# Merging three mixer branches: branch product ahead of its gate, and the branches in another order

## What is computed

```python
def merge_branches(y_pool, y_na, y_mla, g_logits, w_branch, w_out):
    ...
    ys = jnp.stack([y_pool, y_na..., y_mla...], axis=2)
    proj = jnp.einsum('btnc,ncd->btnd', ys, w_branch)
    gates = jax.nn.sigmoid(g_logits.reshape(B, T, N_BRANCHES, D_MODEL))
    return jnp.sum(gates * proj, axis=2) @ w_out
```

## Time and profile before

| what | us |
|---|---|
| median of three runs | 2220.57 (2215.8 to 2220.63) |
| the profiled execution's own time | 2216.48 |
| span of its trace, first to last instruction | 2214.3 |
| TensorE busy in that span | 1944.2 (88%) |

### The profile page before, as it was taken

How to read it: one execution, slowest core, us unless ns; L and a number is a source line. 1 busy time by engine, 2 the same in 40 slices (tenths; PEclk the granted TensorE clock), 3 DMA queues, 4 the chain that set the end, 5 groups by cost and what they waited for, 6 DMA issues and landing times.

```text
span 2214.3 us, 29157 instructions
## 1 busy us (share of the span) xinstructions
PE 1944.2 (88%) x11852; PEld 1507.2 (68%) x11852; DVE 747.4 (34%) x1370; ACT 525.0 (24%) x873; POOL 204.9 (9%) x204
## 2 busy tenths in 40 slices
PE   3799898989999996999718998989899999979990
PEld 1698555668888654888518975656788885558880
DVE  1422657641222135111162227566312122341113
ACT  1311351541111020111142114335311101201113
POOL 0102410010000000100130041100100000001004
PEclk8799999999999998999958999999999999989995
DMA  9413442121132418999672123121213124389985
GB/s 313 161 60 79 156 161 77 58 77 57 58 112 79 124 61 310 358 356 358 227 257 79 69 42 136 39 77 58 77 58 114 58 76 133 131 307 353 359 302 189
DMA packets 183336, 340.97 MB, mean 154 GB/s; under 512 B 12252, under 2 KB 91500, under 8 KB 182892
## 3 DMA queue, kind: packets, MB, share of 16 engines
q1 hardware_dynamic: 152188, 266.16, 34.7%
q10 hardware_dynamic: 23264, 44.96, 6.2%
q0 software_dynamic: 7776, 28.32, 3.6%
HBM read 309.63 MB, written 41.30 MB: 158 GB/s over the span
## 4 chain that ended last, share of the span: by engine, by line
PE 78%; DVE 10%; issue 4%; DMA 3%; ACT 2%; POOL 1%; SPq 0%; ACTq 0%; DVEq 0%; POOLq 0%
PE pair L1491 70%; PE opair L1491 5%; PE pair L1537 3%; DVE mid L1079 1%; DMA r<-mod_rows 1%; DMA ring<-in_w_up 1%; DVE mid L973 1%; DVE mid L975 1%; DVE r L1330 1%; ACT r L879 1%; DVE r_r L1165 1%; DVE mid L1091 0%; DVE mid L1203 0%; ACT mid L846 0%; POOL ysT L1456 0%
## 5 line engine op out<-in xcount | busy, mean ns | idle before, releaser
L1491 PE MATMUL pair<-r_r,mid_r 128*128 128x320 f32 (+2 forms) x2688 | 477.6, 314 | 0.0
L1491 PEld LDWEIGHTS pair<-r_r,mid_r 128*128 128x128 f32 x2688 | 416.6, 189 | 8.8 <-issue 1.5
L1491 PE MATMUL pair<-r,ring 128*128 128x128 f32 (+1 forms) x2432 | 323.6, 294 | 4.5 <-DMA ring<-in_w_up 4.5
L1491 PEld LDWEIGHTS pair<-r,ring 128*128 128x128 f32 x2432 | 299.6, 194 | 38.3 <-issue 15.3
L1491 PE MATMUL pair<-ring,hT 128*128 128x512 f32 (+1 forms) x640 | 231.0, 520 | 5.7 <-DVE hT L1181 3.6
L1537 PE MATMUL pair<-cst,mid 128*128 128x128 f32 (+1 forms) x668 | 106.2, 298 | 122.1 <-DVE mid L975 93.6
L1537 PEld LDWEIGHTS pair<-cst,mid 128*128 128x128 f32 (+1 forms) x668 | 81.1, 151 | 166.4 <-DVE mid L975 97.7
L1491 PEld LDWEIGHTS pair<-ring,hT 128*128 128x128 f32 x640 | 120.4, 190 | 108.5 <-issue 72.7
L1491 PE MATMUL pair<-ysT_r,mid_r 128*128 128x256 f32 (+1 forms) x768 | 171.2, 314 | 11.2 <-issue 11.2
L814 ACT ACTIVATE r<-pair 128x640 f32<-128x640 f32 x48 | 33.7, 703 | 461.9 <-PE pair L1491 461.9
L1491 PE MATMUL pair<-ysT,ring 128*128 128x320 f32 x512 | 143.0, 432 | 0.0
(11 more groups left out here) (230 smaller groups left out, 2137.3 us busy)
## 6 DMA issues: line engine op xcount, KB each, us to landing
ring<-in_w_mod SPq DMA_DIRECT2D x27, 2048.0 KB, 8.9
ring<-in_w_in SPq DMA_DIRECT2D x20, 2048.0 KB, 8.5
ring<-in_w_gate SPq DMA_DIRECT2D x34, 1024.0 KB, 7.3
ring<-in_w_up SPq DMA_DIRECT2D x34, 1024.0 KB, 12.4
ring<-in_w_down SPq DMA_DIRECT2D x34, 1024.0 KB, 11.0
expert_out<-r ACTq DMA_DIRECT2D x34, 512.0 KB, 7.4
ring<-in_w_branch SPq DMA_DIRECT2D x12, 1024.0 KB, 7.4
expert_out<-in_zeros SPq DMA_DIRECT2D x17, 512.0 KB, 12.2
```

The source lines that it names most:

```text
L1491: return nc.tensor.matmul(out, lhsT, rhs, start=first, stop=last, skip_group_check=True)
```

## The change

In each pair TensorE now makes the branch tile first and the gate tile second, and the three branches are taken in the order neighbourhood (1), latent (2), pool (0). The order of the chunks in each group stays gate, then branch. A line was added near the top, so that from there on every line of the new file stands one further down (L814 is L815).

```diff
-MERGE = [(m, n) for c in range(2) for n in range(3) for m in range(4 * c, 4 * c + 4)]
+BRANCHES = (1, 2, 0)
+MERGE = [(m, n) for c in range(2) for n in BRANCHES for m in range(4 * c, 4 * c + 4)]
...
     for m, n in MERGE:
-        jobs += [("gate", m, n), ("branch", m, n)]
+        jobs += [("branch", m, n), ("gate", m, n)]
...
-HALVES += [(("gate", c, n), a, ("gate", 4 * c + 2 * a + 1, n)) for c in range(2) for n in range(3) for a in range(2)]
+HALVES += [(("gate", c, n), a, ("gate", 4 * c + 2 * a + 1, n)) for c in range(2) for n in BRANCHES for a in range(2)]
...
-        for n in range(3):
+        for n in BRANCHES:
             chunks += [(("gate", c, n), None), (("branch", c, n), ("branch", 4 * c + 3, n))]
...
-                await_job(act, ("gate", KD - 1, 2))
+                await_job(act, ("gate", KD - 1, BRANCHES[-1]))
...
-                    out = mergedT[:, m, :] if n == 0 else prod[:, i % 2, :]
+                    out = mergedT[:, m, :] if n == BRANCHES[0] else prod[:, i % 2, :]
...
                     if n == 0 and m == 0:
-                        pe.wait_ge(g_parts_ready, KD)
-                    channels_split(("gate", m, n), HALF_OF[(("gate", m // 4, n), m % 4 // 2)], m % 2 * P, by_channel)
-                    if n == 0 and m == 0:
                         await_read(pe, ("pool", NM - 1))
                     if n == 2 and m == 0:
                         pe.wait_ge(o_freed, 2 * NM)
                     channels(("branch", m, n), wb, (m % 4) * P, NM, yT[n], T, MID)
+                    if n == BRANCHES[0] and m == 0:
+                        pe.wait_ge(g_parts_ready, KD)
+                    channels_split(("gate", m, n), HALF_OF[(("gate", m // 4, n), m % 4 // 2)], m % 2 * P, by_channel)
```

More of the change, by code:

```diff
@@ L565, in _ @@
                             await_mod_stored(sp, n - 1)
-                            await_job(sp, ("gate", KD - 1, 2))
+                            await_job(sp, ("gate", KD - 1, BRANCHES[-1]))
                         for i in range(MT):
@@ L1175, in _ @@
                     await_read(dve, ("gate", m, n))
-                    out = mergedT[:, m, :] if n == 0 else prod[:, i % 2, :]
+                    out = mergedT[:, m, :] if n == BRANCHES[0] else prod[:, i % 2, :]
                     V.tensor_tensor(out, ps[:, MID:MID + T], sig[:, i % 2, :], ALU.mult)\
                         .then_inc(freed[PAIR_OF[("branch", m, n)]], 1)
-                    if n:
+                    if n != BRANCHES[0]:
                         await_read(dve, ("branch", m, n))
                         ins = V.tensor_tensor(mergedT[:, m, :], mergedT[:, m, :], prod[:, i % 2, :], ALU.add)
-                        if n == 2:
+                        if n == BRANCHES[-1]:
                             ins.then_inc(merged, 1)
```

## The result

The changed kernel takes 2224.49 us (median of 9 executions, 2221.05 to 2227.27) against 2217.13 (9 executions, 2215.37 to 2220.63) for the kernel before. The ratio is 1.0028, 95% interval 1.0017 to 1.0039: 6.2 us slower, between 3.8 and 8.6. That is inside the predicted range and inside the 0.3%, and clear of zero. It is not the +1.0 of the likeliest case. The shown execution has a span of 2222.5 us, 8.2 more than that of before.

The account below looks back on a forecast made before the run. TensorE, busy for 88% of the span and without gaps inside the merge, bounds the kernel. Merge end +0.49 us a layer, other terms 0, gives +1.0 over two layers: 2220.57 + 1.0 = 2221.6 us, range 2215.5 to 2226.

Parts of the forecast that it names:

- the likeliest case: Whole kernel: clock kept and everything else hidden, +1.0 us over two layers; chance 0.62.
- What bounds the kernel, and no gain inside the merge: Inside the merge: TensorE fully busy, buffers freed with 2.27 us to spare, weight chunks no gain; term 0.
- End of the merge, +0.49 us a layer: Before y(0): sigmoid and hop now follow the last tile, +0.74, less 0.25; gap from 1.78 to 2.52 us.
- the -0.25 of the last tile: Merge end: TensorE's last matmul ends earlier, a gate tile running 0.16 past the next tile's start, a branch tile 0.41.
- Start of the merge, 0: First tiles: branch tile first hides nothing, moved waits cost nothing; term 0, bounds -0.2 and +0.2.
- The rival's gain: Merge start: the branch tile fills the 5.48 us gap, up to 4.06 us a layer, 2213.5; chance 0.03.
- Transfers, 0: Behind the merge: thirteen issues move by 4.08 us, their users by 0.49; thinnest margin 0.5 us; term 0.
- the clock kept: At y(0) and y(1): the clock stays at 1.00 behind the longer gap, everything else hidden; chance 0.62.
- The rival with both falls: At y(0): clock falls in both layers, 1.7 us each, 2225.0; one or both falls together had chance 0.25.

Follow-up runs that it names:

- the repetition: The changed kernel measured and traced again with no edit, against the kernel before: 1.0022, +4.9 us.
- the shifted kernel: Kernel before plus one useless fp32 matmul of 512 columns inside the merge, after 12 of 24 pairs, no gap changed: 1.0020, +4.4 us.
- the two with the earlier start of the merge: Changed kernel and kernel before, each with y(0) waiting tile by tile and VectorE reading modulation product 5 earlier: 0.9935 and 0.9962 of the kernel before.

## Why the prediction was right in its range and wrong in its size

- **What bounds the kernel, and no gain inside the merge.** Held: both windows are full, the buffers are freed in time, and no tile waits for a weight chunk.
- **End of the merge, +0.49 us a layer.** Held: the gap grew by 0.80 (0.74 predicted), which with the -0.25 of the last tile is +0.55. The way from the first tile to y(0) grew by 0.39 and 0.41, as 0.16 came off at the start.
- **Start of the merge, 0.** Held within its bounds. The prediction let the first branch tile bear the 0.16 us that the first gate tile loses (7.60 for 7.44), but it took 4.47, like every other. The rival's gain is real only when another edit moves the gap of 5.5 us away, and is then 2.8 us a layer.
- **Transfers, 0.** Held. They were issued 3.5 us later relative to y(0). Once the 2 MB chunk had gone ahead it landed in 9.5 us for 19.9, and the modulation rows in 9.9 to 12.2 for 11.3 to 15.8. The residual's eight transfers did not land sooner, as the prediction had it (median 7.1 us for 6.9). L1212 had 5.8 us to spare (757.41 + 12.2 = 769.6, used at 775.44), where the prediction left 0.5; 1.7 of that is the slower y(0). For chunk and rows this agrees with the turns between queues that the Trainium skill describes (DMA: Bandwidth & Descriptors, "Queues, rings and completion order").
- **The step that failed: "the clock kept", given 0.62.** The term was priced rightly as a rival, 1.7 us a layer, and weighed wrongly. In the two traces of the changed kernel the clock fell at four of four places. The argument against it was that dense tiles stand on both sides of the gap. The experiment with a longer gap in the old order shows that they don't prevent it: 2.63 us between the same dense tiles brought the fall in both layers. The Trainium skill (TensorE: Matmul & The Clock Gate, "HAM oscillation — how this bites in real kernels") warns that waits between bursts of matmuls bring the half clock back. It has longer waits in view than these 2.58 us, so it could not have settled the step either way; the traces do. With both falls the sum is 1.0 + 3.4 = +4.4, inside both intervals.
- **What the prediction didn't have at all**: that a fall avoided in one place can come back in another. With the gap filled or closed, and nothing changed ahead of the merge, the tail stretch rose by 1.65 us a layer.
- **Luck in the number.** The rival with both falls ended at 2225.0, and 2224.49 was measured. But it stood on the median of three runs, 2220.57, and the nine gave 2217.13; on that base the same sum is 2221.5, 3 us under the measurement. The range's lower end holds a slip as well: 2221.6 less 4 and less twice 0.2 is 2217.2, not 2216. The measurement lies inside either way.

Open: the rest between 4.2 or 4.4 us and the first measurement's 6.2 is inside its interval, and the repetition gave 4.9, so I look for no other cause. What exactly puts the clock's fall at one place or another isn't settled. Position in time is the reading that fits the shifted kernel and the two with the earlier start of the merge. But the shifted one showed it in one layer only, the kernel with a gap of 2.58 us and the old branch order showed 0 and 3.06 us in its two layers, and no run moved a gap step by step to see where the fall begins.

## What to carry to other kernels

When a kernel lives on TensorE, price a longer gap in front of dense matmuls twice: its own length, and the 1.7 us of a fall of the clock behind it; here the gap grew by 0.80, and the second was about twice that. One of the eight places with a longer gap had no fall, so it is a risk and not a certainty. Look for the consumer's wait, too: an accumulation that waits for each of its inputs in turn, instead of for all, made the order of the last two tiles indifferent for the gap. And when a closed gap brings nothing, compare the length of every later busy stretch with that of before; the loss was in a stretch whose waits hadn't changed. As the position of a stretch seems to decide, what a gap is worth in one kernel may not hold after the next edit ahead of it.

## What was not expected of the hardware

Gaps of 2.58 and 2.63 us in front of y(0) were followed by a fall of the clock from 2.4 to 1.2 GHz in seven of eight places (four traces, two layers each): six cost 1.70 us, the seventh 3.06, and the eighth nothing. Gaps of 1.78 us had none behind them in eight of eight places. Two matmuls of no use, 1.98 us in a gap of 2.1, kept the clock up through a stretch of thin products and were worth 3.3 us a layer. And single traces can differ by almost 5 us ahead of the place of a change (the first merge began at 472.74 us in the kernel before and at 477.56 in the changed one, with the same instructions ahead of it, and at 475.06 in the changed one's second trace), as much as the effect that was looked for.
